# Where sixteen small DMA copies are issued, when a shared buffer is loaded, and where the late transposes stand: two transformer blocks on one core

## The reference

```python
h = rmsnorm(x, ffn_pre_norm[i])
f = (jax.nn.silu(h @ w_gate[i]) * (h @ w_up[i])) @ w_down[i]      # hidden width 2816
x = x + rmsnorm(f, ffn_post_norm[i])
e = rmsnorm(p[i] @ w_ple_proj[i], ple_norm[i])
x = x + jax.nn.sigmoid(x @ w_ple_gate[i]) * e
```

```python
bidx = jnp.maximum(rel, -MAX_REL) + MAX_REL
bias = rel_bias[:, bidx].astype(jnp.float32)
s = jnp.einsum('bqhd,bkhd->bhqk', qb, kb).astype(jnp.float32) * scale + bias[None]
```

## Time and profile before

| | |
|---|---|
| time, median of three runs | 1946.78 us (1946.54 to 1947.69) |
| profiled execution | 1946.78 us, span 1945.0 us |
| mean granted clock of PE | 0.999 |
| PE busy | 1925.1 us, 99% |
| DVE, ACT, POOL busy | 63%, 46%, 28% |
| DMA | 229.70 MB, 118 GB/s over the span |
| chain that ended last | PE 94%, DVE 3%, ACT 2% |

### The profile page before, as it was taken

The page is one execution under the profiler, slowest core; times in us unless marked ns, Lnnn a source line. Parts: engine busy times, 40 slices in busy tenths (PEclk is TensorE's granted clock), DMA queues, the critical chain, the costliest instruction groups (busy, mean ns, idle before and its releaser), DMA issues.

```text
span 1945.0 us, 23730 instructions
## 1 busy us (share of the span) xinstructions
PE 1925.1 (99%) x9278; PEld 1605.7 (83%) x9278; DVE 1226.0 (63%) x1697; ACT 898.4 (46%) x1309; POOL 536.3 (28%) x396
## 2 busy tenths in 40 slices
PE   8999999999999999999999999999999999999998
PEld 7777878888888888888888888888888888888886
DVE  6657676538236845545455857667666676766757
ACT  7445543424235442525255544434455555444435
POOL 2333552251415435353533000000333341000000
PEclk9999999999999999999999999999999999999999
DMA  5312356575532323231315657364322226746553
GB/s 165 95 44 76 101 122 161 136 150 141 101 108 87 109 66 109 66 108 65 108 65 152 155 154 188 109 184 120 108 86 86 86 66 184 181 122 173 127 176 87
DMA packets 164690, 229.70 MB, mean 118 GB/s; under 512 B 4784, under 2 KB 108976, under 8 KB 164464
## 3 DMA queue, kind: packets, MB, share of 16 engines
q1 hardware_dynamic: 148192, 195.24, 32.7%
q0 software_dynamic: 16096, 32.01, 9.5%
q10 hardware_dynamic: 304, 1.12, 0.2%
HBM read 223.23 MB, written 4.72 MB: 117 GB/s over the span
## 4 chain that ended last, share of the span: by engine, by line
PE 94%; DVE 3%; ACT 2%; issue 0%; DMA 0%; SPq 0%; POOL 0%; ACTq 0%; DVEq 0%
PE ps L1150 30%; PE ps L1151 29%; PE ps L1152 29%; PE ps L1322 1%; PE ps L1352 1%; PE ps L1361 1%; PE ps L1362 1%; ACT scr L2255 1%; PE ps L1339 1%; PE ps L1855 0%; DVE x L3243 0%; DMA raw<-in_w_in 0%; DVE hid_lo L3089 0%; DVE hn_lo L3247 0%; ACT w_hi L2008 0%
## 5 line engine op out<-in xcount | busy, mean ns | idle before, releaser
L1150 PE MATMUL ps<-hn_hi,w_hi 128*128 128x512 f32 (+1 forms) x1556 | 607.6, 391 | 4.0 <-DVE hn_lo L3192 1.7
L1152 PE MATMUL ps<-hn_hi,w_lo 128*128 128x512 f32 (+1 forms) x1556 | 599.5, 385 | 0.0
L1151 PE MATMUL ps<-hn_lo,w_hi 128*128 128x512 f32 (+1 forms) x1556 | 599.4, 385 | 0.0
L1004 POOL TENSOR_TENSOR w_lo<-raw,w_hi 128x512 fp32r<-128x512 f32 x244 | 343.0, 1438 | 517.8 <-ACT w_hi L2000 517.8
L1150 PEld LDWEIGHTS ps<-hn_hi,w_hi 128*128 128x128 f32 x1556 | 292.7, 188 | 66.4 <-issue 4.8
L1152 PEld LDWEIGHTS ps<-hn_hi,w_lo 128*128 128x128 f32 x1556 | 292.5, 188 | 59.3
L1151 PEld LDWEIGHTS ps<-hn_lo,w_hi 128*128 128x128 f32 x1556 | 292.8, 188 | 57.2 <-issue 1.4
L1150 PE MATMUL ps<-w_hi,hid_hi 128*128 128x512 f32 x616 | 240.0, 390 | 0.2
L1151 PE MATMUL ps<-w_lo,hid_hi 128*128 128x512 f32 x616 | 239.7, 389 | 0.0
L1152 PE MATMUL ps<-w_hi,hid_lo 128*128 128x512 f32 x616 | 239.7, 389 | 0.0
L2044 ACT ACTIVATE w_hi<-raw 128x1024 fp32r<-128x1024 f32 x112 | 116.1, 1055 | 205.7 <-PE ps L1152 205.4
(11 more groups left out here) (383 smaller groups left out, 2902.7 us busy)
## 6 DMA issues: line engine op xcount, KB each, us to landing
raw<-in_mlp_w SPq DMA_DIRECT2D x56, 1024.0 KB, 5.5
raw<-in_ret_w_in SPq DMA_DIRECT2D x24, 1024.0 KB, 5.1
aux<-in_mlp_w POOLq DMA_DIRECT2D x16, 1024.0 KB, 9.2
raw<-in_att_w_in SPq DMA_DIRECT2D x12, 1024.0 KB, 5.3
raw<-in_w_gate SPq DMA_DIRECT2D x11, 1024.0 KB, 5.4
raw<-in_w_up SPq DMA_DIRECT2D x11, 1024.0 KB, 5.3
raw<-in_w_down SPq DMA_DIRECT2D x9, 1024.0 KB, 5.2
raw<-in_ret_w_out SPq DMA_DIRECT2D x8, 1024.0 KB, 5.1
```

The costliest lines, as they stand in the source:

```text
L1004: ins = pool.tensor_tensor(w_lo[:, slot, at], raw[:, slot, at], w_hi[:, slot, at].bitcast(F32), ALU.subtract)
L1150: pe.matmul(o, hi, rhs_hi, start=start, stop=False, skip_group_check=True)
L1151: pe.matmul(o, hi, rhs_lo, start=False, stop=False, skip_group_check=True)
L1152: return pe.matmul(o, lo, rhs_hi, start=False, stop=stop, skip_group_check=True)
```

## The change

Four things are changed. The copies `spread_ext` are issued by ACT instead of SP, with ACT waiting for `ext_built` instead of SP: in groups 0 and 1 two, two and one after the first three pairs of blocks, in group 2 two after each of its three pairs. In group 0, the load into `s3_m_s4`, with the wait for `apart_sum`, stands after block 3's load instead of block 5's (in group 1 it stood there already). PE does `turn_back(1)` before `gate_half(1, 0)`, which is no longer cut in two. ACT scales the late rows before it splits gate chunk 1.

```diff
-            def spread_ext(n):
-                sp.dma_start(ext_rows[n], ext[n:n + 1, :].unsqueeze(1).to_broadcast([1, 64, EXT]))\
-                    .then_inc(s["ext_out"], 16)
...
-            sp.wait_ge(s["ext_built"], 3)
             for g in range(3):
                 for j in range(2, FFN.UPS[g]):
                     load_ffn_up(g, j)
-                    spread_ext(6 * g + j - 2)
-                    if g < 2 and j == (5, 3)[g]:
+                    if g < 2 and j == 3:
                         if g == 0:
                             sp.wait_ge(s["apart_sum"], 2)
...
             gate_half(0, 0)
-            gate_half(1, 0, range(4))
             turn_back(1)
-            gate_half(1, 0, range(4, KD))
+            gate_half(1, 0)
             gate_half(0, 1)
             gate_half(1, 1)
...
+            def spread_ext(n):
+                act.dma_start(ext_rows[n], ext[n:n + 1, :].unsqueeze(1).to_broadcast([1, 64, EXT]))\
+                    .then_inc(s["ext_out"], 16)
...
                 if (g, j) == (0, 0):
                     rsqrt(N_FFN, D)
+                    act.wait_ge(s["ext_built"], 3)
                     act.preload_act_table_set("silu_and_others")
...
                     if g == 0 and 1 <= j < 3:
                         for t in range(4 * j - 4, 4 * j):
                             square(N_PLE, t, e_buf[:, t, :], tmp)
+                    if j < 3:
+                        for n in range(2 * j, min(2 * j + 2, 5)):
+                            spread_ext(5 * g + n)
...
             for j in range(3):
                 ffn_gate_up(2, j)
+                for n in range(2):
+                    spread_ext(10 + 2 * j + n)
                 act.wait_ge(pair_free[1], FFN.taken_pair(2, j, 1))
...
             ffn_back_hi(0, 3)
+            ffn_row_scaled(1)
             split(GATE.chunk(1))
-            ffn_row_scaled(1)
```

More of the change, by code:

```diff
@@ L1656, in _, with gate_half @@
             ffn_end_right()
-            def gate_half(m, half, ks=range(KD)):
+            def gate_half(m, half):
                 c, g, tokens = GATE.chunk(m), GATE.group(m), (EARLY_TOKENS, LATE_TOKENS)[half]
@@ L1662, in gate_half @@
                 wait = parts_ready(c, 11 + 3 * m)
-                if half == 0 and ks[0] == 0:
+                if half == 0:
                     group_empty(g)
                     pe.wait_ge(s["ffn_taken"], FFN.taken(2, FFN.RIGHT + (1, 3)[m]))
-                for k in ks:
+                for k in range(KD):
                     if half == 0:
@@ L1674, in gate_half @@
                                     hn_lo[:, k, tokens], half == 0 and k == 0, k == KD - 1)
-                if half and ks[-1] == KD - 1:
+                if half:
                     ins.then_inc(s["group_done"], 1)
```

## The result

The kernel after takes 1959.62 us (median of four runs, 1959.3 to 1960.18), the kernel before 1946.66 us beside it: ratio 1.0065 (95% interval 1.005 to 1.0081), 13.0 us slower. The forecast was 1954.4, range 1949.0 to 1957.2: the sign was right, the time lies outside the range. The profiled execution took 1959.2 us, span 1957.3 (before 1945.0).

A forecast was written before the change was run, and what follows sets the result against it. The prediction took TensorE (PE) to bound the kernel and summed 0 (SP) + 0 (ACT's issues) + 5.3 (block 4) + 2.3 (gate) = 7.6 us onto 1946.8, forecasting 1954.4 us, range 1949.0 to 1957.2.

The forecast's parts named there:

- What bounds the kernel: Whole kernel: TensorE (PE), busy 1925.1 of 1945.0 us; a change costs whatever PE comes to wait for.
- SP's part: SP stands for `apart_sum` until about 270.2, then issues three loads; the 16 copy issues it saves gain nothing.
- ACT's issues: ACT's 16 added copy issues, 0.60 us each, stay hidden in its waits: cost 0, at most 1.2 us once.
- It holds them 2.9 us: Group 0: one `ext` copy holds the DMA engines 2.9 us, read from the window 274.5 to 277.4.
- 278.1 + 2 x 2.9 = 283.9: Block 4's landing time: 278.1 behind the `aux` load, then held up by both `ext` copies in full; stall 5.3 us.
- My upper bound: Block 4's latest landing, 285.0, by adding the 6.9 us delay of a load beside a POOL accumulation; stall 7.1 us.
- rival B: Behind block 4's stall TensorE's clock falls, matmuls 0.43 us apart, 0.8 to about 3 us lost: 1956.3; chance 0.22.
- The gate: Gate chunk 1: PE waits for ACT's scaling, then POOL's first quarter; loss 2.3 us, between 2.1 and 2.7.
- rival D: Block 4 in time and the transposes fill PE's waits at the gate: 1946.6, or 1944.5; chance 0.04.
- A: The `ext` copies don't hold up block 4, which lands at 278.1; only the gate's loss is left, 1949.1; chance 0.17.
- C: The next two copies, about 293, eat the slack of block 6's load: 3 to 4 us more, 1958; chance 0.07.
- E: `apart_sum` comes before 263.73, so SP doesn't stand and the change doesn't do what it says; excluded by DVE's row.

The follow-up runs named there:

- experiment 1: Kernel after, with only the `aux` load of group 0 put back behind block 5's load: 1950.28 us, ratio 1.0015.
- experiment 2: Kernel before, with only the `aux` load of group 0 put ahead of block 4's load: 1946.89 us, ratio 0.9997.
- experiment 4: Kernel after, with the first two `ext` copies of group 0 moved on ACT from pair 0 to pair 2: 1958.36 us, ratio 1.0059.
- experiment 7: Kernel after, with the first two `ext` copies issued by SP, between the `aux` load and block 4's: 1960.99 us, ratio 1.007.
- experiment 6: Kernel after, with `ext` copy 0 issued early, before ACT's rounding of block 2, and copy 1 left behind pair 0: 1954.11 us, ratio 1.0034.
- 9: Kernel before, with only ACT's order at the gate changed, late rows scaled ahead of the split of chunk 1: 1953.13 us, ratio 1.0028.
- experiment 8: Kernel before, with only PE's order at the gate changed, late transposes ahead of `gate_half(1, 0)`: 1947.58 us, ratio 1.0003.
- experiment 10: Kernel after, with 30 unread matmuls of 128x512 put in front of PE's wait for block 4: 1958.43 us, ratio 1.0052.
- experiment 5: Kernel after, with the first two `ext` copies issued some 18 us earlier on ACT, before its rounding of block 2: 1951.01 us, ratio 1.0019.

## Why the prediction was wrong

**What bounds the kernel, SP's part, ACT's issues: right.** No new wait of PE appeared outside the two places. SP stood for `apart_sum` and then issued three loads; its freed time gave nothing. ACT's issues cost next to nothing where they stand (+0.14 us in experiment 1). The delay by the `aux` load alone was 7.3 us forecast and 7.7 to 7.8 measured, and did not reach PE (experiment 2).

**The step that failed: "It holds them 2.9 us", and from it "278.1 + 2 x 2.9 = 283.9".** The mechanism is the one forecast, and both edits are needed for it, but the pair held block 4 for 8.3 us and not 5.8. I had taken a copy's price from the window of the earlier trace rows, 2.9 us at 46 GB/s: 133 KB, which I read as most of one copy's 160 KB. A copy alone moves 28 GB/s (experiments 4 and 7), so 46 GB/s must have held bytes of a load, and the window was only the part of the copy with little beside it. The trace of the kernel before shows this too, in a narrower window between the two loads:

```profile
275.00:277.00 2.00, 2.00 (x10) 1.65 (x10) 1.46 (x1) 2.00 (x2) 0.00 (x0) 1.00 0.90 33
```

At 33 GB/s a copy takes 160 / 33 = 4.8 us, and two of them would hold block 4 for some 9.7, an estimate on the safe side of the 8.3. In the way of block 4, one copy costs 2.9 us. That this is just the number I had is luck: the copy of experiment 6 was issued at 273.61 and landed 7.9 us later, the loads still moved 367 GB/s from 275.6 to 278.2, and only from 278.2 to 280.6 did the rate fall to 68. So about half of it lay beside other loads. The second copy costs 16.0 - 10.6 = 5.4, nearly a full 5.7. Why it finds less cover is not shown: with both under way the windows still move 62 to 108 GB/s, more than the copies' 28, so bytes of loads went beside them. My upper bound (285.0, from the delay by a POOL accumulation) was too low too: block 4 landed at 285.8 in a program that ran 0.8 us ahead. From landing to PE the chain was as forecast: 290.53 - 285.8 = 4.7 us, against 4.6. The stall became 8.06 us instead of 5.3: +2.8, of which 2.5 are the copies' (8.3 for 5.8) and the rest the later base (7.7 for 7.3).

**The clock: rival B happened, on top.** I gave it 0.22 and priced it between 0.8 and 3 us. It cost 2.04 us after, and came in every run in which PE waited long: 2.5 us (experiment 6), 3.9 (9), 6.4 (4), 7.9 (after) and 9.1 (7). After the waits of 1.3 us at block 3 and at the gate, of 1.5 us in experiment 8, and of 1.7 us at 189 us of the kernel before, it did not come. The Trainium skill (TensorE: Matmul & The Clock Gate, Part 1) has it that the clock follows how busy PE has been of late, so that an idle PE loses the full clock and must work for a while to regain it. The windows agree, with 0.50 to 0.52 through the end of the wait and the first ten matmuls, and experiment 10 removes it. I weighed it as a possibility beside a forecast; it belonged in the sum as soon as that sum held a wait of 5 us. My evidence against it, that a wait of 1.3 us had left the pace alone, said nothing of a wait four times as long.

**The gate: right.** +2.58 us, bounds 2.1 to 2.7, I took 2.3. Both waits (0.69 and 1.32) came as worked out, and POOL kept the slower of the two paces considered, which puts the loss near the upper bound; rival D is out, since the first quarter was late for the end of the transposes.

**Rivals A, C and E.** A fails at block 4 (landing 16.0 us, not 8). C needed the next copies to make block 6 late: no such wait exists. E is out too: SP stood until 269.39.

**The sum with what was measured:** 8.06 + 2.04 + 2.58 = 12.7 instead of 7.6, which gives 1959.5 from 1946.8. The range ended at 1957.2 because it took the stall's upper bound from the wrong kind of transfer, and never put a larger stall and the clock in one case, though both come from the same wait.

## What to carry to other kernels

A small DMA is priced by how long it keeps the DMA engines, not by its bytes: divide its size by the rate that it has with nothing beside it. That is its price at most; beside loads that hide part of it, one copy cost 2.9 us instead of 5.7. Moving it to another engine's queue changes when it starts and little of what it takes from the others (8.3 us against 9.5), so ask which load has its turn then. Put a DMA that is far from its deadline where no load with little slack follows: experiment 5 did it, and experiment 4 shows that later is no such place by itself. And when a sum puts a long wait on TensorE in a busy stretch, add the matmuls that run at half clock behind it: here waits of 2.5 us and more cost 1.5 to 2.0 us extra, and waits of 1.7 us and less cost none.

## What the hardware showed beyond this

- A copy that reads one row of 2,560 bytes in one partition 64 times runs at 28 GB/s with the DMA engines 93% busy, against 350 to 410 GB/s for a weight load.
- Issuing a DMA can take long on the issuing engine when other DMAs stand ahead in its queue. In experiment 7 SP's two loads behind the copies took 3.28 and 6.15 us to issue, against 0.37 to 0.58:

```profile
272.34 3.28 SPq L842 DMA_DIRECT2D raw<-in_w_gate  x1
275.67 6.15 SPq L842 DMA_DIRECT2D raw<-in_w_up  x1
```

- That the queue was full is a guess from the load and the copies ahead of them; no row shows it. On ACT the three issues of experiment 4 took 4.28 us, where two took 1.24 in the kernel after.
- The clock need not be low when PE comes back: in experiments 6 and 9 the first two or three matmuls were 0.31 and 0.29 us apart (of 128x256: 0.19 and 0.12), and the slow pace began 0.4 to 0.6 us behind the wait.
